# Routing the 64 sample tokens one head at a time on 64 partitions instead of two heads at a time on 128

## What is computed

```python
q = (xb @ w_query).reshape(tokens, 8, 2, 128)             # 8 heads, two halves
s = einsum('thpc,hpkc->thpk', q, sub_keys)                # 128 scores per half
top_s, top_i = top_k(s, 16)                               # best 16 of each half
cand_s = top_s[:, :, 0, :, None] + top_s[:, :, 1, None, :]  # 256 pairs
best_s, best_j = top_k(cand_s, 16)                        # best 16 pairs
experts = ...                                             # their 16 expert numbers
gate = softmax(best_s)                                    # over the 16 of a head
act = gelu(einsum('td,tkd->tk', xb, expert_u[experts]))   # 128 experts per token
out = einsum('tk,tkd->td', gate * act, expert_v[experts])
y = layer_norm(ALPHA * x1 + out)
```

## Time and profile before

| | |
|---|---|
| median of 3 runs | 3554.06 us (3552.52 to 3568.26) |
| time of the profiled execution | 3554.06 us |
| its span, first to last instruction | 3552.2 us |
| TensorE busy | 2509.4 us (71% of the span) |
| VectorE busy | 2759.7 us (78%) |
| ScalarE busy | 680.7 us (19%) |
| GpSimd busy | 1270.4 us (36%) |
| moved by DMA | 1394.02 MB, mean 392 GB/s |

### The profile page before, as it was taken

The page is one execution under the profiler, slowest core; times in us unless marked ns, Lnnn a source line. Parts: engine busy times, 40 slices in busy tenths (PEclk is TensorE's granted clock), DMA queues, the critical chain, the costliest instruction groups (busy, mean ns, idle before and its releaser), DMA issues.

```text
span 3552.2 us, 39353 instructions
## 1 busy us (share of the span) xinstructions
PE 2509.4 (71%) x13744; PEld 1155.7 (33%) x13744; DVE 2759.7 (78%) x7340; ACT 680.7 (19%) x1477; POOL 1270.4 (36%) x1092
## 2 busy tenths in 40 slices
PE   7965468425766776677668766876697667779976
PEld 5434235421233223332333233323233322223421
DVE  5179747899889977997899789978997894445865
ACT  1210122102210321032103210420043001221010
POOL 0022112223443444344444443444444333224342
PEclk7987678757888888898889988998899878889999
DMA  9998897998999999999999999999999999999997
GB/s 336 360 352 315 319 352 276 394 374 328 421 420 391 384 421 421 414 391 420 421 417 403 421 421 408 388 421 421 415 396 421 421 408 422 419 420 400 419 421 328
DMA packets 218502, 1394.02 MB, mean 392 GB/s; under 512 B 27384, under 2 KB 38136, under 8 KB 66616
## 3 DMA queue, kind: packets, MB, share of 16 engines
q0 software_dynamic: 156672, 1140.92, 78.6%
q1 hardware_dynamic: 40080, 141.80, 10.8%
q10 hardware_dynamic: 21552, 108.79, 7.8%
HBM read 1378.32 MB, written 80.04 MB: 411 GB/s over the span
## 4 chain that ended last, share of the span: by engine, by line
DVE 40%; DMA 24%; PE 23%; issue 10%; ACT 2%; POOL 1%; SPq 0%; ACTq 0%; POOLq 0%; DVEq 0%
DMA t<-in_expert_uv,t 22%; DVE t L1062 13%; PE psum L1426 7%; PE psum L1264 6%; DVE t L929 4%; PE psum L1342 4%; DVE psum L1089 3%; DVE t L1074 2%; PE psum L1371 2%; DVE t L1010 2%; DVE t L1008 2%; DVE t L1011 2%; DVE t L1009 2%; POOL t L616 1%; DVE t L1007 1%
## 5 line engine op out<-in xcount | busy, mean ns | idle before, releaser
L616 POOL DMA_INDIRECT t<-in_expert_uv,t x1088 | 1270.2, 1167 | 2248.9 <-PE psum L1422 860.4
L1426 PE MATMUL psum<-t,t 64*64 64x512 f32 x4576 | 1275.6, 695 | 677.3 <-DVE t L1074 675.5
L1062 DVE CUSTOM_DVE_ANT_0 t<-t,t 128x1024 f32<-128x1024 f32 x1088 | 1321.0, 1222 | 454.2 <-DMA t<-in_expert_uv,t 433.6
L1426 PEld LDWEIGHTS psum<-t,t 64*64 64x64 f32 x4576 | 320.7, 149 | 1457.6 <-DVE t L1074 853.1
L1422 PE MATMUL psum<-t,t 64*64 64x512 f32 x2592 | 780.1, 730 | 0.0
L775 ACT ACTIVATE t<-t 128x2 f32<-128x2 f32 x544 | 110.6, 203 | 1971.5 <-DVE t L1062 1938.2
L1371 PEld LDWEIGHTS psum<-t,t 128*128 128x128 f32 x2304 | 292.9, 210 | 73.3 <-issue 58.6
L1371 PE MATMUL psum<-t,t 128*128 128x128 f32 (+1 forms) x2304 | 303.6, 295 | 8.8 <-ACT t L738 6.5
L1264 PE MATMUL psum<-t,t 128*128 128x128 f32 (+2 forms) x768 | 264.2, 505 | 7.4 <-DMA t<-in_xT 6.3
L929 DVE SCALAR_TENSOR_TENSOR t<-t,t,t 128x128 f32<-128x128 f32 x840 | 238.2, 346 | 0.0
L1422 PEld LDWEIGHTS psum<-t,t 64*64 64x64 f32 x2592 | 176.9, 152 | 0.1
(11 more groups left out here) (139 smaller groups left out, 2111.2 us busy)
## 6 DMA issues: line engine op xcount, KB each, us to landing
t<-in_wq_t ACTq DMA_DIRECT2D x72, 1024.0 KB
out<-in_cache_k_win SPq DMA_DIRECT2D x8, 4080.0 KB
out<-in_cache_v_win SPq DMA_DIRECT2D x8, 4080.0 KB
t<-in_w_in_t ACTq DMA_DIRECT2D x44, 512.0 KB, 7.3
t<-in_kc_t SPq DMA_DIRECT2D x8, 2560.0 KB
t<-in_vc_t SPq DMA_DIRECT2D x8, 2560.0 KB
t<-in_expert_uv,t POOLq DMA_INDIRECT x1088
t<-in_w_v_t ACTq DMA_DIRECT2D x6, 1024.0 KB, 7.3
```

Source lines behind the costliest of these rows:

```text
L616: pool.indirect_dma_start(ring[:, r, :], None, I["expert_uv"], bass.IndirectOffsetOnAxis(ap=idn[t % 2][:, s:s + 1], axis=0)).then_inc(land ...
L1062: dve.tensor_tensor_reduce(out=ring[:, r, 0:D], in0=x1[t % 2][:, :], in1=ring[:, r, 0:D], scale=1.0, scalar=0.0, op0=ALU.mult, op1=ALU.add ...
L1426: last = pe.matmul(MAIN[t][half][NS * a:NS * a + NS, :], zt[NS * a:NS * a + NS, k % Z_RING, j, :], vv[NS * a:NS * a + NS, :], start=(c == ...
```

## The change

The sample tile's heads are no longer paired. Each of its 8 heads gets key scores, a copy of the scores, and a routing of its own, on the 64 partitions of the 64 tokens (`r = rows(m)` in the place of `r = P`). The four pieces of head `h` now stand at the steps `96 + 4 * h` plus 0, 1, 2 and 3. So that a gather still fetches 128 rows, the second 8 of a head's 16 expert numbers are then copied by DMA from partitions 0 to 63 to partitions 64 to 127, into the columns of the first 8, and the same is done with the gates, four heads at a time. There are again 64 slots: slot `s` is head `s // 8`, rank `s % 8` on the lower and `8 + s % 8` on the upper partitions, which `column` translates to a column of `idn`, `gtn` and `dots`. GpSimd waits for the copied numbers of a head (`id_up`) before its first gather, and VectorE for the copied gates (`gate_up`) before `weigh` uses them. The SyncE queue gets 10 more DMAs (8 of numbers, 2 of gates) behind the copy of `x1`. The gates are computed for 4 heads at a time.

```diff
+        def column(t, s):
+            return s if t < PT else s // PH * TOP + s % PH
...
-        SHARED = [h // 2 + PH // 2 * (h % 2) for h in range(PH)]
...
                     sp.dma_start(x1[PT % 2][NS:P, :], x1[PT % 2][0:NS, :]).then_inc(x1_up, 16)
+                    for h in range(PH):
+                        sp.wait_ge(a_route, PH * PT + h + 1)
+                        sp.dma_start(idn[PT % 2][NS:P, h * TOP:h * TOP + PH], idn[PT % 2][0:NS, h * TOP + PH:(h + 1) * TOP]).then_inc(id_up[h], 16)
+                        if h % 4 == 3:
+                            g4 = gtn[PT % 2].rearrange("p (h k) -> p h k", h=PH)
+                            sp.wait_ge(a_gate, gate_events(PT, h // 4))
+                            sp.dma_start(g4[NS:P, h - 3:h + 1, 0:PH], g4[0:NS, h - 3:h + 1, PH:]).then_inc(gate_up[h // 4], 16)
...
-                if s % TOP == 0:
+                if s % TOP == 0 and t < PT:
                     pool.wait_ge(a_route, PH * t + s // TOP + 1)
+                elif t == PT and s % PH == 0:
+                    pool.wait_ge(id_up[s // PH], 16)
...
-            def score_pair_copy(j):
-                act.wait_ge(a_s, PH * PT + 2 * j + 2)
-                if j >= 2:
-                    act.wait_ge(a_route, PH * PT + j - 1)
-                act.activation(sh[:, j % 2, :], bank[4 + j % 2][:, 0:2 * NK], ACT.Copy).then_inc(a_sc, 1)
...
-                        if g % 2 and h % 2:
-                            score_pair_copy(h // 2)
-                        elif g % 2 == 0:
+                        if g % 2:
+                            score_copy(PT, h)
+                        else:
                             query_copy(PT, h)
...
             def route_side(m, h, side):
-                r = P
+                r = rows(m)
...
+                if t == PT and c % (2 * PH) == 0:
+                    dve.wait_ge(gate_up[c // (2 * PH)], 16)
                 dve.wait_ge(a_gelu, gelus(t, c) + 1)
...
                 if g >= 24:
-                    j, at_ = divmod(4 * (g - 24) + i, 8)
-                    if at_ in (0, 2):
-                        route_side(PT, j, at_ // 2)
-                    if at_ == 4:
-                        route_pairs(PT, j)
-                    if at_ == 6:
-                        route_experts(PT, j)
+                    if i < 2:
+                        route_side(PT, g - 24, i)
+                    elif i == 2:
+                        route_pairs(PT, g - 24)
+                    else:
+                        route_experts(PT, g - 24)
                 if g == 27 and i == 3:
-                    gates(PT, range(2))
+                    gates(PT, range(4))
...
-            def key_scores_pair(j):
-                pe.wait_ge(a_qc, PH * PT + 2 * j + 2)
-                if j >= 2:
-                    pe.wait_ge(a_sc, PH * PT + j - 1)
-                else:
-                    pe.wait_ge(x1_done, 2 * PT + j + 1)
-                for a in range(2):
-                    h = SHARED[2 * j + a]
-                    for side in range(2):
-                        last = pe.matmul(bank[4 + j % 2][NS * a:NS * a + NS, side * NK:(side + 1) * NK], qh[:, a, side * NS:(side + 1) * NS], skT[:, 2 * h + side, :], start=True, stop=True)
-                    last.then_inc(a_s, 1)
...
-                        if g % 2 and h % 2:
-                            key_scores_pair(h // 2)
-                        elif g % 2 == 0:
+                        if g % 2:
+                            key_scores(PT, h)
+                        else:
                             queries(PT, h)
```

More of the change, by code:

```diff
@@ L406, in build @@
         x1_up = sem("x1_up")
+        id_up = [sem(f"id_up{h}") for h in range(PH)]
+        gate_up = [sem(f"gate_up{i}") for i in range(2)]
         landed = [sem(f"landed{i}") for i in range(RING)]
@@ L616, in gather @@
                 pool.indirect_dma_start(ring[:, r, :], None, I["expert_uv"],
-                                        bass.IndirectOffsetOnAxis(ap=idn[t % 2][:, s:s + 1], axis=0)).then_inc(landed[r], 16)
+                                        bass.IndirectOffsetOnAxis(ap=idn[t % 2][:, column(t, s):column(t, s) + 1], axis=0)).then_inc(landed[r], 16)
             for t in range(TILES):
@@ L718, in route_loads @@
                 for h in (0, 1):
-                    act.dma_start(wq[:, h % 2, :, :], I["wq_t"][h if m < PT else SHARED[h]]).then_inc(wq_in[h % 2], 16)
+                    act.dma_start(wq[:, h % 2, :, :], I["wq_t"][h]).then_inc(wq_in[h % 2], 16)
             def conv_swish(m):
@@ L750, in query_copy @@
                 if h < PH - 2:
-                    act.dma_start(wq[:, h % 2, :, :], I["wq_t"][h + 2 if m < PT else SHARED[h + 2]]).then_inc(wq_in[h % 2], 16)
+                    act.dma_start(wq[:, h % 2, :, :], I["wq_t"][h + 2]).then_inc(wq_in[h % 2], 16)
             def score_copy(m, h):
@@ L757, in score_copy @@
                 act.activation(sh[0:rows(m), h % 2, :], bank[4 + h % 2][0:rows(m), 0:2 * NK], ACT.Copy).then_inc(a_sc, 1)
-            def score_pair_copy(j):
-                act.wait_ge(a_s, PH * PT + 2 * j + 2)
-                if j >= 2:
-                    act.wait_ge(a_route, PH * PT + j - 1)
-                act.activation(sh[:, j % 2, :], bank[4 + j % 2][:, 0:2 * NK], ACT.Copy).then_inc(a_sc, 1)
             def gate_exp(m, event, heads):
                 act.wait_ge(a_diff, event)
-                g_ = gtn[m % 2][:, heads.start * TOP:heads.stop * TOP]
+                g_ = gtn[m % 2][0:rows(m), heads.start * TOP:heads.stop * TOP]
                 act.activation(g_, g_, ACT.Exp).then_inc(a_exp, 1)
@@ L772, in gelu @@
                 act.wait_ge(a_dot, SLOTS * t + w * (c + 1))
-                s = w * c
+                s = column(t, w * c)
                 d_ = dots[t % 2][:, s:s + w]
@@ L878, in _ @@
                         if g == 28 and i == 0 and m == PT:
-                            gate_exp(PT, gate_events(PT, 0), range(2))
+                            gate_exp(PT, gate_events(PT, 0), range(4))
                         if g == GROUPS - 1 and i == 3 and m == PT:
-                            gate_exp(PT, gate_events(PT), range(2, 4))
+                            gate_exp(PT, gate_events(PT), range(4, PH))
                         if g == GROUPS - 1 and i == 1 and n in AUX_TILES:
@@ L1042, in gates @@
             def gates(m, heads):
-                r, n_ = P, len(heads)
+                r, n_ = rows(m), len(heads)
                 g3 = gtn[m % 2][0:r, heads.start * TOP:heads.stop * TOP].rearrange("p (h k) -> p h k", h=n_)
@@ L1062, in dot @@
                 dve.tensor_tensor_reduce(out=ring[:, r, 0:D], in0=x1[t % 2][:, :], in1=ring[:, r, 0:D], scale=1.0,
-                                         scalar=0.0, op0=ALU.mult, op1=ALU.add, accum_out=dots[t % 2][:, s:s + 1]).then_inc(a_dot, 1)
+                                         scalar=0.0, op0=ALU.mult, op1=ALU.add, accum_out=dots[t % 2][:, column(t, s):column(t, s) + 1]).then_inc(a_dot, 1)
             def weigh(t, c):
                 k = pair(t, c)
-                s = 2 * c
+                s = column(t, 2 * c)
                 d2, g2 = dots[t % 2][:, s:s + 2], gtn[t % 2][:, s:s + 2]
+                if t == PT and c % (2 * PH) == 0:
+                    dve.wait_ge(gate_up[c // (2 * PH)], 16)
                 dve.wait_ge(a_gelu, gelus(t, c) + 1)
@@ L1166, in sample_front @@
                 if g >= 24:
-                    j, at_ = divmod(4 * (g - 24) + i, 8)
-                    if at_ in (0, 2):
-                        route_side(PT, j, at_ // 2)
-                    if at_ == 4:
-                        route_pairs(PT, j)
-                    if at_ == 6:
-                        route_experts(PT, j)
+                    if i < 2:
[4 more added lines that the diff above has]
+                        route_experts(PT, g - 24)
                 if g == 27 and i == 3:
-                    gates(PT, range(2))
+                    gates(PT, range(4))
                 if g == 28 and i == 3:
-                    gates_end(PT, gate_events(PT, 0), range(2))
+                    gates_end(PT, gate_events(PT, 0), range(4))
                 if g == 31 and i == 3:
-                    gates(PT, range(2, 4))
-                    gates_end(PT, gate_events(PT), range(2, 4))
+                    gates(PT, range(4, PH))
+                    gates_end(PT, gate_events(PT), range(4, PH))
             def front(m, g, i):
```

## The result

The changed kernel is slower: 3591.89 us median (3580.90 to 3596.64, 6 runs) against 3554.26 us, a ratio of 1.0089 with a 95% interval of [1.0068, 1.0108]. A second measurement of the same two kernels gave 3581.45 against 3554.78 us, 1.0071 [1.0049, 1.0093]. The profiled execution took 3579.77 us, 25.7 us more than that of before; why the first median lies 12 us higher is taken up at the end of the experiments. Lines in the code have moved: the dot is L1067 (was L1062), the weighing L1078 and L1081, a routing L1012 to L1044, GpSimd's gathers L627.

A forecast was written before the change was run, and what follows sets the result against it. DMA gathers bound the kernel, with VectorE binding from step 97 of phase 7 after the change. 40.7 us of routings - 8.6 of waits - 5 given back + 0 for copies = +27.1 us on 3554.06, so 3581.2 us; range 3569 to 3593.

The forecast's parts named there:

- sum of 27.1 us: Whole kernel: 40.7 us of routings, less 8.6 of vanished waits and 5 given back, copies at 0: +0.76%.
- Nothing less for the DMA engines: Sample tile: still 64 gathers of 128 rows, so the change removes nothing that the DMA engines carry.
- copies, key scores, ScalarE at nothing: Phase 7: ten copies taken as 0 (bounds 0 to 10 us), 16 matmuls either way, ScalarE only 1.5 us more.
- Four more routings: VectorE in phase 7: eight routings for four at 10.18 us each, 40.7 us more, nothing saved by half the partitions.
- Waits that vanish: VectorE in phase 7 from step 97 on: its waits for gathers go, 8.6 us in 8 pieces.
- Give-back: Start of phase 8, up to slot 12: a fuller ring saves 1.2 to 7.2 us, taken as 5.
- eight slots landed at the end of phase 7: End of phase 7: slots 0 to 7 of the sample tile have landed, where before only about two had.
- my bound: Slot 12's gather, issue to landing without a backlog: between 3.4 us and the first gather's 9.4 us; near the low end taken.
- Phase 8 from there on at 2.50 us a gather: Phase 8 from slot 12 on: the 51 gathers take 127.6 us as before, 2.50 us each.
- Rival (A): Phases 7 and 8: the ring of gathers hides the routings, 0 to 3 us, about 3556 us; 12% together with a half-way case.
- Rival (B): Phase 7: new ScalarE waits for routings or TensorE at a lower clock, the whole 40.7 us, 3594.8 us; 12%.
- Rival (C): Sample tile: gathers start sooner after one routing, at most 8.6 us faster, 3545.5 us; 3%.

The follow-up runs named there:

- e3: The kernel before plus only the ten small copies, into tiles that nobody reads: 3554.02 us, 0.9993.
- e4: The changed kernel with the routing of heads 1, 3, 5 and 7 left out, each taking over the numbers of the head before: 3553.95 us, 0.9994.
- e2: The kernel before, on 128 partitions and in pairs, with every piece of the sample tile's four paired routings done twice: 3584.31 us, 1.0074.
- e1: The changed kernel once more without an edit, against the kernel before: 3581.45 us, 1.0071.
- e10: The changed kernel once more without an edit, one execution: 3602.39 us.
- e5: The kernel before with only the eight side pieces of the paired routing done twice: 3560.55 us, 1.0023.
- e6: The kernel before with the eight side pieces and the four pair pieces of the paired routing done twice: 3574.05 us, 1.0058.
- e9: The changed kernel with five routings in phase 7 and three in phase 8, these from its step 26 on: 3557.43 us, 1.0011.
- e8: The changed kernel with five routings in phase 7 and three in phase 8, these from its step 12 on: 3560.66 us, 1.0009.

## Why the prediction was right

The median of 3591.89 us lies in the range of 3569 to 3593, near its upper end, and the profiled execution's 3579.77 us beside the forecast 3581.2. The mechanism held: VectorE's four more routings in phase 7, less the waits that they fill. Two things were luck. The median is inside the range though 8 to 10 us of its +37.6 are not in the stretches of the change. And the sum of 27.1 us met the measured 27.5 because its errors cancel: 38.5 - 10.0 - 0.9 = 27.6 us for 40.7 - 8.6 - 5. Step by step, in the profiled pair:

- **Nothing less for the DMA engines; copies, key scores, ScalarE at nothing**: right. The copies alone cost nothing (e3), the change without the extra routings neither (e4).
- **Four more routings, 40.7 us**: 38.5 measured (28.5 of A, and the 8.6 + 1.4 us of waits that vanished). Half the partitions do save something, some 8 ns of an instruction and about 1.7 us over the eight routings (e2); I had taken nothing.
- **Waits that vanish, 8.6 us**: all of them, and 1.4 us of the wait for the exponential at the end of phase 7 (1.7 us before, now 0.3), which I had not counted since the exponential was to stand where it stood.
- **Give-back, 5 us**: the term that was mis-sized. It is 0.9 us in the profiled execution, and over before, after, e1, e2 and e10 B lies between 153.6 and 156.0 us, so nothing within the scatter. Two steps of the reckoning were off. First, I counted eight slots landed at the end of phase 7 for about two before; it was about six for four. The gather of slot 4 was issued only at 3399.8 us, after 9.1 us of waiting for TensorE to free a slot, and the DMA engines still worked until about 3413 us; then they stood idle for over 3 us (0.59, 0.00 and 0.73 in the windows). The two gathers more are 4.8 us of transfer; some 2 us more of idle time in B took part of it back (the queues' shares in B sum to 97.1% for 98.5%), and lower rates most of the rest. Second, slot 12 was the wrong place to look for it: VectorE waited only 0.50 us for that gather before, so it was its own chain of work and not the gathers that held it until 26.9 us, and no more than 0.5 us could be won there. After the change it took slot 12 up at 28.1 us without a wait. The first slot that it waited for was 15, issued at 3432.34 and used at 3441.57 us, 9.2 us later: near the first gather's 9.4 us, the end of my bound that I had set aside.
- **Phase 8 from there on at 2.50 us a gather**: right, from slot 15 on (48 gathers in 120.0 us). So was what the stretch shows: DMA share 0.86 for a forecast of 0.85, rate 338 for 355 GB/s, A 124.8 us for 128.
- **Rival (A), the ring hides it**: fell, but it has a grain of truth: the first 9 to 12 us of extra VectorE time are free (e5, e6). **Rival (B)**: its waits of ScalarE are there (7.3 us), and TensorE's last pair of the phase ran at a lower granted clock (0.50, its 1.2 GHz level, from 3406 to 3412 us, TensorE having stood idle from 3403.2 to 3408.6 us; the pair took 5.50 us for 3.65). DVE waited 2.2 us for it instead of 0.7, as bounded. The first costs nothing; the second, 1.5 us, stands inside B. **Rival (C)**: no sign of it.

The Trainium skill's page "Trainium Kernel Development and Optimization", section Best Practices, says to tile always to 128 partitions. The trace agrees: 8 half-filled routings took nearly twice the time of 4 full ones (8 x 9.99 for 4 x 10.18 us).

## What to carry to other kernels

In this kernel an instruction on 64 partitions costs what one on 128 costs, less 7 to 9 ns, so packing two heads on the partitions halves a chain of VectorE instructions, and undoing it doubles the chain. What that is worth is read from the stretch in which the chain stands: the extra time is free as far as it fills waits for transfers (8.6 us here, with at most a few us of backlog), and beyond that it costs about one for one. The same work put where the engine has caught up with its transfers costs next to nothing (e9, +1.8 us for 30 us of work); its first part put where the engine is still catching up costs in full (e8, 10.4 us for the 10 us of four pieces). And before a term of a sum is placed at an event, look at how long the engine waited there: a gather that is waited for 0.5 us can give back 0.5 us at most.

## What the runs showed of the hardware

The copies of 2 KB between partitions landed 6.0 us after issue, and 6.7 us beside full DMA engines (e3), where ten such small ones cost nothing. A gather whose transfer takes 2.5 us was used 9.2 us after its issue, in engines that were at work again after a pause of some 3 us. VectorE's top-8 search over 128 scores takes 280 ns on 64 partitions and 287 on 128. And in some executions one load of 316 KB, issued the same way, was used 21.5 to 24.0 us after its issue instead of 10.5 to 12.1, which makes a prompt phase about 10 us longer.
